# Expert weights in 8 KB runs per partition: a hybrid mLSTM, dilated attention and MoE layer in fp32 on one Trainium2 core

## The reference, cut to what matters

```python
def moe(u, router_w, router_b, w_gate, w_up, w_down):      # w_gate, w_up (16, 1024, 512), w_down (16, 512, 1024)
    xt = u.reshape(B * S, D)
    scores = jax.nn.sigmoid(xt @ router_w)                  # router_w (1024, 16)
    ...                                                     # top 2 of the best group of 4, weights "combine"
    for e in range(N_EXPERTS):
        he = jax.nn.silu(xt @ w_gate[e]) * (xt @ w_up[e])
        out = out + combine[:, e:e + 1] * (he @ w_down[e])

u = modulate(rms_norm(x, norm_ffn_g[l]), sh_f, sc_f)        # h * (1 + scale) + shift, per channel
x = x + gt_f[:, None, :] * moe(u, ...)
return rms_norm(x, final_norm_g)
```

## Time and profile before

| | |
|---|---|
| runs | 627.28, 630.81, 630.83 us; median 630.81 |
| the profiled execution | 629.4 us, span 627.7 us, so 1.7 us lie around the span |
| busy | PE 584.9 us (93%), PE weight loads 432.7 (69%), DVE 315.6 (50%), ACT 228.9 (36%) |
| chain that ended last | PE 81%, DMA 9%, DVE 4%, ACT 2%, SP's queue 2% |
| expert chunks, median from issue to landing | gate 14.6 us, up 14.2, down 14.4 |
| granted TensorE clock | 0.987 of full speed over the span |

### The profile page before, as it was taken

The page is one execution under the profiler, slowest core; times in us unless marked ns, Lnnn a source line. Parts: engine busy times, 40 slices in busy tenths (PEclk is TensorE's granted clock), DMA queues, the critical chain, the costliest instruction groups (busy, mean ns, idle before and its releaser), DMA issues.

```text
span 627.7 us, 8391 instructions
## 1 busy us (share of the span) xinstructions
PE 584.9 (93%) x3564; PEld 432.7 (69%) x3564; DVE 315.6 (50%) x464; ACT 228.9 (36%) x310; POOL 5.6 (1%) x13
## 2 busy tenths in 40 slices
PE   2599999999999999999999999989999999999784
PEld 0599988999998888999999886533543533533232
DVE  3797976756568876787463755403202122220203
ACT  4425647444455455476542444201201111110103
POOL 3000000000000000000000000000000000000000
PEclk9799999999999999999999998999999999999997
DMA  8996664785758945734599798299999999999991
GB/s 316 362 387 219 202 202 135 273 289 199 277 199 306 368 166 203 268 105 171 196 363 360 273 391 323 75 400 387 401 387 401 387 402 387 401 387 401 387 353 68
DMA packets 80584, 184.77 MB, mean 294 GB/s; under 512 B 5561, under 2 KB 5665, under 8 KB 78497
## 3 DMA queue, kind: packets, MB, share of 16 engines
q1 hardware_dynamic: 78018, 184.06, 79.7%
q10 hardware_dynamic: 2528, 0.16, 0.3%
HBM read 183.16 MB, written 1.05 MB: 293 GB/s over the span
## 4 chain that ended last, share of the span: by engine, by line
PE 81%; DMA 9%; DVE 4%; ACT 2%; SPq 2%; issue 1%; DVEq 0%; ACTq 0%
PE ps L1334 29%; PE ps L1342 16%; PE ps L1545 14%; PE ps L1557 7%; DMA ring<-in_w_down_e_dram 3%; DMA ring<-in_w_gate_e_dram 2%; DMA ring<-in_w_up_e_dram 2%; DMA raw<-in_w_in_dram 2%; PE ps L1581 2%; PE ps L1533 2%; DVE acc_a L800 1%; PE ps L1409 1%; SPq L440 1%; PE ps L1504 1%; PE ps L1448 1%
## 5 line engine op out<-in xcount | busy, mean ns | idle before, releaser
L784 DVE TENSOR_TENSOR lo<-raw,hi 128x2048 fp32r<-128x2048 f32 x52 | 118.8, 2290 | 45.8 <-ACT hi L532 45.3
L1334 PE MATMUL ps<-u_hi,hi 128*128 128x256 f32 x432 | 124.0, 287 | 1.1 <-DVE u_lo L850 1.1
L1334 PE MATMUL ps<-u_hi,lo 128*128 128x256 f32 x432 | 122.2, 283 | 0.0
L1334 PE MATMUL ps<-u_lo,hi 128*128 128x256 f32 x432 | 122.2, 283 | 0.0
L1545 PE MATMUL ps<-ring,xe_t 128*64 128x512 f32 x512 | 113.8, 594 | 7.7 <-DMA ring<-in_w_up_e_dram 4.0
L532 ACT CAST hi<-raw 128x2048 fp32r<-128x2048 f32 x52 | 98.8, 1907 | 51.6 <-PE ps L1334 24.6
L1545 PEld LDWEIGHTS ps<-ring,xe_t 128*64 128x64 f32 x512 | 37.5, 137 | 75.4 <-issue 75.3
L1334 PEld LDWEIGHTS ps<-u_hi,hi 128*128 128x128 f32 x432 | 82.8, 192 | 1.4 <-DVE u_lo L850 1.3
L1334 PEld LDWEIGHTS ps<-u_lo,hi 128*128 128x128 f32 x432 | 82.8, 192 | 0.1
L1334 PEld LDWEIGHTS ps<-u_hi,lo 128*128 128x128 f32 x432 | 82.8, 192 | 0.0
L1557 PE MATMUL ps<-ring,he_t 128*64 128x512 f32 x256 | 57.1, 596 | 1.5 <-DMA ring<-in_w_down_e_dram 0.7
(11 more groups left out here) (288 smaller groups left out, 811.2 us busy)
## 6 DMA issues: line engine op xcount, KB each, us to landing
raw<-in_w_in_dram SPq DMA_DIRECT2D x42, 1024.0 KB, 5.2
ring<-in_w_gate_e_dram SPq DMA_DIRECT2D x32, 1024.0 KB, 14.6
ring<-in_w_up_e_dram SPq DMA_DIRECT2D x32, 1024.0 KB, 14.2
ring<-in_w_down_e_dram SPq DMA_DIRECT2D x32, 1024.0 KB, 14.4
raw<-in_ada_w_dram SPq DMA_DIRECT2D x16, 1024.0 KB, 5.2
first_ada<-in_ada_w_dram SPq DMA_DIRECT2D x16, 512.0 KB, 11.8
raw<-in_w_branch_m_dram SPq DMA_DIRECT2D x4, 1024.0 KB, 5.6
raw<-in_w_out_dram SPq DMA_DIRECT2D x4, 1024.0 KB, 7.6
```

What stands on the lines that cost most here:

```text
L784: V.tensor_tensor(lo[b % RING][:], src[:], hi[b % RING][:].bitcast(F32), ALU.subtract).then_inc(lo_ready, 1)
L1334: ins = mm(dst, w[:, k, cols], x[:, k0 + k, :], start=(first and c % 2 == 0 and k == 0 and n == 0), stop=(end and k == KB - 1 and n == 2), ...
```

## The change

Channel `512 h + 4 p + i` is now on partition `p`, in half `h`, place `i`, so that a half of an expert's gate or up matrix is 4 neighbouring rows per partition, 8 KB in one run. For down (512 rows) it is row `256 h + 2 p + i`, again 8 KB in one run. Everything that pairs with these weights follows: the router's weights, the ffn norm's weights (loaded straight to the partitions, no longer turned with the other rows), the columns, the residual's turns, the gather and the turns of `he`. A new helper `near` gives the strided slice. Its step is 4 elements of 4 bytes in the columns, the residual's turns and the gather, and 2 elements in the turns of `he`. These slices are the stationary operands. The number of instructions on PE, ACT and DVE stays, and so does the number of DMA issues.

```diff
+def near(start, kk, k):
+
+    return slice(start + kk // k * k * P + kk % k, start + (kk // k + 1) * k * P, k)
...
-        vec = small("vec", [P, 104])
+        vec = small("vec", [P, 96])
...
+        ffn_g = small("ffn_g", [P, 2, KB])
...
                 matrix, half = PARTS[part]
-                w = matrices[matrix][(2 * p + e) % NE].rearrange("(k p) n -> p k n", p=P)
-                k = w.shape[1] // 2
-                sp.dma_start(ring[slot][:].rearrange("p (k n) -> p k n", k=k), w[:, half * k:(half + 1) * k, :]
-                             ).then_inc(ring_loaded[slot], 16)
+                w = matrices[matrix][(2 * p + e) % NE].rearrange("(h p k) n -> p h (k n)", h=2, p=P)
+                sp.dma_start(ring[slot][:], w[:, half, :]).then_inc(ring_loaded[slot], 16)
...
-            act.dma_start(rows[96:104, :], A["norm_ffn_g"][0].rearrange("(c p) -> c p", p=P)).then_inc(rows_loaded, 16)
+            act.dma_start(ffn_g[:], A["norm_ffn_g"][0].rearrange("(h p k) -> p h k", h=2, p=P)).then_inc(rows_loaded, 16)
...
-            act.dma_start(rw[:], A["router_w"].rearrange("(k p) n -> p k n", p=P)).then_inc(small_loaded, 16)
+            act.dma_start(rw[:].rearrange("p (h k) n -> p h (k n)", h=2), A["router_w"].rearrange("(h p k) n -> p h (k n)", h=2, p=P)).then_inc(small_loaded, 16)
...
-                    event(V.tensor_copy(vec[:], ps[0][:, 0:104]), "vec")
+                    event(V.tensor_copy(vec[:], ps[0][:, 0:96]), "vec")
...
-                    step(V.scalar_tensor_tensor(out=ffn_col[:, 1, :], in0=ps[6][:, KT:2 * KT], scalar=1.0, in1=vec[:, 96:104],
+                    step(V.scalar_tensor_tensor(out=ffn_col[:, 1, :], in0=ps[6][:, KT:2 * KT], scalar=1.0, in1=ffn_g[:].rearrange("p h k -> p (h k)"),
...
-            event(tr(ps[0][:, 0:104], rows[0:104, :], ident[0:104, 0:104]), "vec_t")
+            event(tr(ps[0][:, 0:96], rows[0:96, :], ident[0:96, 0:96]), "vec_t")
...
-                                    tr_ins = tr(ps[6][:, c * P:(c + 1) * P], x_res[:, 0, NB + c * P:NB + (c + 1) * P], ident[:])
+                                    tr_ins = tr(ps[6][:, c * P:(c + 1) * P], x_res[:, 0, near(NB, c, KB)], ident[:])
...
-                        ins = mm(ps[6][:, KT * m + k:KT * m + k + 1], mod[:, 1 + m, k * P:(k + 1) * P], ones[:, 0:1],
+                        ins = mm(ps[6][:, KT * m + k:KT * m + k + 1], mod[:, 1 + m, near(0, k, KB)], ones[:, 0:1],
                                  start=True, stop=True)
...
-                            ins = tr(ps[4 + t][:, k * P:(k + 1) * P], x_res[:, t, k * P:(k + 1) * P], ident[:])
+                            ins = tr(ps[4 + t][:, k * P:(k + 1) * P], x_res[:, t, near(0, k, KB)], ident[:])
...
-                ins = tr(ps[7][:, k * P:(k + 1) * P], x_res[:, 1, NB + k * P:NB + (k + 1) * P], ident[:])
+                ins = tr(ps[7][:, k * P:(k + 1) * P], x_res[:, 1, near(NB, k, KB)], ident[:])
...
-                            ins = mm(dst, x[:, t, kk * P:(kk + 1) * P], onehot[:, t, 0:cols],
+                            ins = mm(dst, x[:, t, near(0, kk, KB)], onehot[:, t, 0:cols],
...
-                    ins = tr(ps[6][:, k * P:(k + 1) * P], he[:, k * P:(k + 1) * P], ident[:])
+                    ins = tr(ps[6][:, k * P:(k + 1) * P], he[:, near(0, k, 2)], ident[:])
```

## The result

The changed kernel takes 642.45 us, the median of 4 runs (641.51 to 642.90), beside 629.99 for the kernel before on the same chip (627.28 to 630.83): a ratio of 1.020, 95% interval 1.0172 to 1.0228. It is slower, by about 2%. The profiled execution took 642.9 us, with a span of 641.0; the clock granted to TensorE was 0.976 in the mean.

A forecast was written before the change was run, and what follows sets the result against it. DMA was taken to bound the kernel's end, with PE's floor limiting the gain: 629.4 - 9.6 + 0 + 0 = 619.8 us, or 621.2 against the median; forecast 620.5 between them, range 616 to 638.

The forecast's parts named there:

- Bound before, floor and ceiling: Expert stage: DMA ends the kernel; PE's floor puts the last down product at 605.69, so at most 9.6 us gained.
- Rate of 8 KB runs: Expert chunk loads: 420 GB/s in place of 387 (gate, up) and 410 (down); low end 410, high end 446.
- the doubt whether the run is the cause of 387: Rival, chance 0.12: something else in the expert stage slows gate and up loads, which reach only 398 GB/s; 625.7 us.
- Strided stationaries: PE's stepped loads in columns, gathers and turns: cost taken as 0; upper bound a load twice as long, 210 ns.
- the rival at 0.22: Chance 0.22: stepped loads take twice as long in columns, residual's turns and gathers, 16.7 us on PE; 636.5 us.
- a load of some 165 ns: PE's stepped loads: the length from which their added time reaches 9.6 us and so decides.
- The start: First loads, `norm_ffn_g` and the router's in other runs: 0 together, bounds -0.5 and +1 us.
- The signs named in advance: Signs of a wrong forecast: columns 16 in 3.4 us, a gather over 7, last product near 622, DMA idle before the end.
- one rule: Trainium skill on stationary loads: 16-byte SBUF lines need two hits for full performance, so a step of 16 bytes pays.

The follow-up runs named there:

- the last two experiments: Kernel before with its contiguous column products issued twice, 637.23 us; changed kernel with its stepped column products in four groups instead of two, 637.55 us.
- the one with both edits: Changed kernel with columns computed from contiguous rows and a mask, and the gather reading tokens that ACT permuted once: 619.63 us, ratio 0.9848.
- the program of its own: Separate list of TensorE products, not the kernel, varying one operand's step, plus ACT and DVE copies; 125 ns a product at steps 1 and 2, 235 at 4.

## Why the prediction was wrong

- **Bound before, floor and ceiling**: right. PE's floor for the last down product was put at 605.69, and the loads alone reached 606.11, 9.14 us earlier than before, under the ceiling of 9.6.
- **Rate of 8 KB runs**: right. 420 was taken, 421 measured, and the doubt whether the run is the cause of 387 is gone. That the figure came out so exactly is in part luck: it rests on two stretches of 2 us, 446 and 410 GB/s, and the stretches just ahead of them (236 to 238 and 134 to 136) read 402 and 379. The Trainium skill (DMA: Bandwidth & Descriptors, section Why small descriptors are slow) gives each packet a fixed cost of some 3 bus cycles; an estimate from its figures is that going from 2 to 8 KB is worth 3.4%. By that rule the trace disagrees, with 421 over 387, 8.8%.
- **Strided stationaries, "I take 0"**: this is the step that failed. What it put at nothing measured 16.3 us, 3.88 in the columns and 12.42 in the gathers. Its reason was that "the load that costs most already goes at half the pace of the transposes' load with the same 4 bytes per column, so reading the element isn't what limits it". From the slower pace of a contiguous load I concluded that the read has slack to spare. It has, in the loads of products: a step of 2 is free. But the slack is used up before 3, and the change steps by 4. The argument could say that there was some slack, never how much, and I read it as enough.
- **Its price, in the rival at 0.22**: right in kind and a little low in both. Priced were 2.7 + 9.0 for the gathers and 3.4 for the columns; measured 3.06 + 3 x 3.12 = 12.42 and 2 x 1.94 = 3.88. The residual's turns were put at 1.6 and cost 0.1 a group of 8 (0.96 for 0.87), since their columns hide the load; `he`'s, put at 0 to 3.4, cost 0.08 for each 4 (0.59 for 0.51), in 8 groups 0.6. Its remark that a step decides from a load of some 165 ns on is a little off: by its own terms 9.6 us are reached at some 170. The loads measured are past either (235 ns a product).
- **What no case had**: the clock. The rival gave 636.5 and the kernel takes 642.45, above the range. From the profiled executions, at the last down product, in order of time: start 0.57, columns 3.88, the blocks behind them at the lower clock 2.92, from there to the first gather 1.78, first gather 3.06, first down product at a clock of 0.81 1.69 (8.78 for 7.09), the other gathers 9.36, turns of `he` 0.6, less the 9.56 of stall: together 14.3, and 14.36 measured (629.61 - 615.25). The 2.92 are shown by the last two experiments to be the long group's doing. The 1.78 are for the most part clock too: 8 of the logits' products took 1.89 us (L1300) at a clock of 0.50, where they took 1.07 at 0.96, and the 8 products behind them took 5.96 (L1510) at 0.60, where they took 5.22 at 0.68, in all 1.56; the stepped turns of the residual are the other 0.2. The steps aren't what lowers it there. The kernel with the old loads, which has every step, took 1.06 and 5.23 for the two, and so did the one with both edits (1.06 and 5.22); the one with the plain gather took 1.30 and 4.97, and the ones with plain columns and with a step of 2 took 1.89 and 6.02, and 1.89 and 6.07. The first down product took 8.78 in six of the seven profiled kernels that turn `he` with a step, among them the one with both edits, whose columns and gathers have none, and 7.09 in the seventh (the plain gather) and in the three whose `he` is turned without a step. Each is one execution, and no run was made to separate them. So that the steps cause these two terms isn't shown, and why they vary stays open.
- **The start**: right, 0 within 0.6. ACT's issue of `norm_ffn_g` took 0.48 us, against 0.51; its load landed later, so that PE's turn of the rows began at 10.01 in place of 8.24, but the reader on DVE came at 12.66, against 12.50. The kernel with the 8 KB loads alone, whose start is as before, is at its columns at 319.38, between 318.99 and 319.56, so the load isn't shown to cost even the 0.57.
- **The signs named in advance** were those that came: columns near 3.4 (3.62), a gather of over 7 (7.72), a last product near 622 (it starts at 622.54 and ends at 629.61), and the DMA idle before the end.

The chance was set wrong with it. No row could speak for a free step of 4, one rule spoke against it, and the price was worked out; the case deserved at least as much as the forecast.

## What to carry to other kernels

A slice with a step as a stationary is an added cost of PE until it has been measured: here 2 elements of 4 bytes were free, a step of 3 made such products 1.4 times as long and one of 4 1.9 times, so choose the dealing of features by the largest step that is free, not by the longest run of the DMA. When one engine's stall is removed, the change pays only with what its other side doesn't spend: work out PE's added time against the stall before counting the DMA's gain. And look at what stands *behind* a lengthened group of small products, since its lower clock can cost nearly as much as the group's added time (2.92 us beside 3.88 here).

## What else the runs showed of the chip

- Runs of 2, 4 and 8 KB per partition give 387, 410 and 421 GB/s in a steady stream of 1 MB loads.
- Behind a group of 3.6 to 4.2 us of one-column products, contiguous or not, TensorE's granted clock was 0.65 to 0.80 over the next block, which then took 7.2 to 8.5 us in place of 5.9 (eight blocks in four kernels); behind groups of 1.7 to 1.8 us it was 1.00.
- In the program of its own a *moving* operand with a step of 2 took 240 ns for 256 columns, as with 4 (243), against 125 contiguous; the same step in the stationary was free.
- There ACT's copy of 512 columns, which has a step of 4 elements on one side or the other, took 1.10 us in place of 0.63, and DVE's two-input operation 1.08 in place of 0.69.
